# A mixer, convolution and MLP kernel: split forget gate, all high parts on ScalarE, another order in the first stage, the first swishes and the modulation

## The reference

```python
h = rms_norm(x, norm_w); proj = h @ w_in
gq, gk, gv, glr, hq, hf, hi, xq, gate = split(proj)
# heads 0-3: gated linear attention, gate from glr; m = rms_norm(mem, mem_norm_w), mk, mv = m @ w_mem_kv
# heads 4-7: the same recurrence; forget gate sigmoid(hf), key (1 - lb) * sigmoid(-hf)
# heads 8-11: cross attention of xq to mk, mv
mixed = concat(heads) * silu(gate)
x = rms_norm(x + mixed @ w_out, final_norm_w)
mod = silu(c) @ w_mod + b_mod            # shifts, scales and gates of the next two blocks
x = x + gate1 * conv_block(modulate(norm(x)))   # 1024->2048, GLU, 31-tap depthwise, LayerNorm, silu, 1024->1024
x = x + gate2 * mlp(modulate(norm(x)))          # hidden 4096
```

## Time and profile before

| | |
|---|---|
| time, median of 3 | 2173.16 us (2172.41 to 2177.71) |
| profiled execution, own time / span | 2175.57 / 2173.8 us |
| PE busy | 2060.9 us (95%) |
| DVE, ACT, POOL busy | 1077.7 (50%), 793.0 (36%), 808.0 (37%) us |
| mean granted PE clock | 0.968 of full speed |
| POOL's high parts, L2534 | 32 of 1134 ns, 36.3 us |
| ACT's high parts, L1715 | 173 of 1058 ns, 183.0 us |
| landing of MODRAW, median | 4.5 us after issue |

### The profile page before, as it was taken

One profiled execution on the slowest core, in us unless ns is written; L12 is line 12 of the kernel. 1 busy time (PEld: TensorE's weight loads), 2 busy tenths in 40 slices (PEclk: granted clock), 3 DMA queues, 4 the chain that ended last, 5 costly groups with the idle time before them and its releaser, 6 DMA issues. The chain is left out here.

```text
span 2173.8 us, 26461 instructions
## 1 busy us (share of the span) xinstructions
PE 2060.9 (95%) x10302; PEld 1727.4 (79%) x10302; DVE 1077.7 (50%) x1881; ACT 793.0 (36%) x1339; POOL 808.0 (37%) x481
## 2 busy tenths in 40 slices
PE   7899999999899899999899998899999999999997
PEld 5788988878887678888778776678777888888886
DVE  6364455446454255555569978994423122122125
ACT  4413221332434522132356556652425333312211
POOL 3342122122131344353238877663443444222220
PEclk9999999999999999999999999899899999999998
DMA  4211101011011486776245432123222333111112
GB/s 166 70 56 49 40 30 49 30 56 32 21 60 43 150 303 209 234 261 204 96 150 190 175 121 82 58 79 96 68 88 88 97 97 97 49 49 49 49 49 78
DMA packets 69420, 215.64 MB, mean 99 GB/s; under 512 B 7712, under 2 KB 8096, under 8 KB 69168
## 3 DMA queue, kind: packets, MB, share of 16 engines
q1 hardware_dynamic: 55184, 187.73, 25.2%
q10 hardware_dynamic: 14112, 26.22, 3.7%
HBM read 184.56 MB, written 29.36 MB: 98 GB/s over the span
## 5 line engine op out<-in xcount | busy, mean ns | idle before, releaser
L1320 PE MATMUL B<-HB,WH 128*128 128x512 f32 x2976 | 950.4, 406 | 28.6 <-ACT WH L1715 10.8
L2536 POOL TENSOR_TENSOR WL<-RAW,WH 128x1024 fp32r<-128x1024 f32 x205 | 496.3, 2424 | 686.2 <-ACT WH L1715 681.9
L1320 PEld LDWEIGHTS B<-HB,WH 128*128 128x128 f32 x2976 | 557.8, 192 | 151.7 <-issue 33.2
L1320 PE MATMUL B<-HB,WL 128*128 128x512 f32 x1488 | 574.1, 396 | 4.1 <-POOL WL L2536 4.0
L1715 ACT ACTIVATE WH<-RAW 128x1024 fp32r<-128x1024 f32 x173 | 183.0, 1058 | 460.8 <-DMA RAW<-wall 444.4
L1320 PEld LDWEIGHTS B<-HB,WL 128*128 128x128 f32 x1488 | 284.9, 191 | 68.2 <-POOL WL L2536 6.6
L2034 DVE SCALAR_TENSOR_TENSOR RES<-B,modv,RES 128x512 f32<-128x512 f32 x144 | 105.1, 748 | 207.6 <-PE B L1499 181.4
L2034 DVE SCALAR_TENSOR_TENSOR B<-UP,vec,B 128x512 f32<-128x512 f32 x308 | 207.4, 750 | 0.0
L1499 PE MATMUL B<-HIDH,WH 128*128 128x512 f32 x512 | 188.2, 401 | 6.5 <-DVE HIDL L2031 5.0
L1499 PE MATMUL B<-HIDL,WH 128*128 128x512 f32 x512 | 183.8, 392 | 0.0
L1499 PE MATMUL B<-HIDH,WL 128*128 128x512 f32 x512 | 183.6, 392 | 0.0
(11 more groups left out here) (240 smaller groups left out, 2688.6 us busy)
## 6 DMA issues: line engine op xcount, KB each, us to landing
RAW<-wall SPq DMA_DIRECT2D x203, 512.0 KB, 3.5
MODRAW<-wmod ACTq DMA_DIRECT2D x96, 256.0 KB, 4.5
WH<-parts SPq DMA_DIRECT2D x32, 512.0 KB, 3.2
WL<-parts SPq DMA_DIRECT2D x32, 512.0 KB, 4.2
RES<-xT SPq DMA_DIRECT2D x16, 512.0 KB, 8.2
oscr<-OT SPq DMA_DIRECT2D x32, 256.0 KB, 2.1
OI<-oscr SPq DMA_DIRECT2D x16, 512.0 KB, 5.2
parts<-WH SPq DMA_DIRECT2D x16, 512.0 KB, 5.2
```

Source lines behind the costliest of these rows:

```text
L1320: i = pe.matmul(bank, a[:, ks], hb(part, k, h), start=k == 0 and n == 0, stop=k == 7 and n == 2)
L2536: po.tensor_tensor(lo, raw, hi.bitcast(F32), ALU.subtract).then_inc(sig[f"w_lo{q % NW}"], 1)
```

## The change

Six edits. (1) The forget gate is two pieces: the sigmoids at once, the scalings 4.0 planner-us later, the head's recurrence 2.5 after that (it was 6.0 in one). (2) All high parts are made by ACT. (3) Stores of turned outputs are a piece of their own, 2.5 planner-us after the turning. (4) In the first stage 20 matmuls on a tile of ones run first (line 1640); the identity is waited for only where it is used; ACT starts one raw load instead of two; steps of the norms of x and mem come earlier or in another order, with double buffers for mem. (5) A gate block's B x R product is a piece `mix_r` of its own; the swishes of blocks 0 and 1 come after the product of block 2. (6) In blocks 4 to 8 `mods(4)` is put in after the first half too, so the 96 pieces run up to 20 ahead of where they stood.

```diff
-FORGET = 6.0
+FORGET = (4.0, 2.5)
-LATER = (2.5, 3.0, 3.0)
+LATER = (2.5, 3.0, 3.0, 2.5)
+WARM = 20
 def u_split():
-            piece("split", q, "act" if UNITS[q][0] in ("mk", "mv") else hi_by[0])
+            piece("split", q)
 def x_stats():
         take(S, "x_sum")
         piece("x_sum")
-        for _ in range(4):
-            yield
-        piece("x_diag")
         yield
         yield
+        piece("x_diag")
+        piece("m_square")
+        for _ in range(3):
+            yield
         for h in range(2):
             take(S, "x_row", h)
             piece("x_row", h)
         R_done[0] = True
+        yield
+        yield
+        for h in range(2):
+            piece("glr", h)
+        for h in range(2):
+            piece("q_out", 0, h)
...
 def turn():
+            while P.kinds["turn_o"] - P.kinds["ot_store"] > 4 - tiles:
+                next_due()
...
+            later(LATER[3], store)
...
 def recurrent(n):
-        piece("forget", n)
-        later(FORGET, lambda: bg.append(linear(n)))
+        piece("forget_sig", n)
+        def forget():
+            piece("forget", n)
+            later(FORGET[1], lambda: bg.append(linear(n)))
+        later(FORGET[0], forget)
...
-    def mix_out(e, h):
+    def mix_out(e, h, first=True):
+        if first:
+            piece("mix_r", e, h)
         piece("mix", e, h)
...
 def mixed(e):
             gate_product(e, h)
             mix_out(e, h)
+            if h == 0 and 4 <= e < 9:
+                mods(4)
...
     gate_product(1, 0)
-    crossed_up_to(1)
     for e, h in ((0, 0), (0, 1), (1, 0)):
-        mix_out(e, h)
+        piece("mix_r", e, h)
     gate_product(1, 1)
-    mix_out(1, 1)
-    for e, h in ((2, 0), (2, 1), (3, 0)):
-        gate_product(e, h)
+    piece("mix_r", 1, 1)
+    for h in range(2):
+        gate_product(2, h)
+    crossed_up_to(0)
+    for e, h in ((0, 0), (0, 1), (1, 0), (1, 1)):
+        mix_out(e, h, False)
+    for h in range(2):
+        piece("mix_r", 2, h)
+        gate_product(3, h)
...
 # PE program
-            w.wait_ge(sig["d_ident"], 16)
+            w.wait_ge(sig["ones"], 1)
+            for _ in range(WARM):
+                pe.matmul(BANKS[use["glr", 0][0]], ones[:, :].bitcast(F32R), ...)
 # SP program
             load_x(0)
             sp.dma_start(vec[:, :], vecs).then_inc(sig["d_vec"], 16)
+            load_x(1)
+            load(1)
+            for k in range(2, 8):
+                load_x(k)
             sp.dma_start(ident[:, :], ident_d).then_inc(sig["d_ident"], 16)
-            for k in range(1, 8):
-                load_x(k)
```

More of the change, by code:

```diff
@@ L180, in make_plan @@
     lanes = {"dve": [], "pool": []}
-    hi_by, ahead, pace = ["act"], [AHEAD], [PASS]
+    ahead, pace = [AHEAD], [PASS]
     def u_split():
@@ L356, in mem_norm @@
         yield
-        yield
-        yield
         piece("m_diag")
-        yield
+        for _ in range(3):
+            yield
         take(S, "m_row")
         piece("m_row")
+        for k in range(8):
+            yield
+            piece("m_tile", k)
     rate[0] = 0.8
@@ L382, in make_plan @@
         step()
+    step_in(bg2)
     for h in range(2):
-        piece("glr", h)
-    for h in range(2):
-        piece("q_out", 0, h)
         piece("k_out", 0, h)
@@ L403, in scale @@
             later(LATER[2], turn)
+        tiles = 2 if n < 4 else 1
         def turn():
-            for f in range(2 if n < 4 else 1):
+            while P.kinds["turn_o"] - P.kinds["ot_store"] > 4 - tiles:
+                next_due()
+            for f in range(tiles):
                 take(S, "turn_o", n, hh, f)
@@ L409, in turn, with store @@
             fin_n[n >= 8, hh] += 1
+            later(LATER[3], store)
+        def store():
+            for f in range(tiles):
+                piece("ot_store", n, hh, f)
         later(LATER[0], rms)
@@ L510, in make_plan @@
             piece("gate_up", h, hf)
+        if bg2:
+            step_in(bg2)
         piece("gate_log", h)
@@ L677, in make_plan @@
         after(2.5 * f, "res_load", f)
[L678 to L681, removed]
+    for h in range(2):
+        mix_out(2, h, False)
+    for h in range(2):
+        mix_out(3, h)
     mods(4)
@@ L1113, in build_program @@
         dg0 = at("p0dg", 1024, F32, x0 + 4 * K4)
-        macc, msq, mdg, mtm = (at(f"mem{i}", 256, F32, x0 + 8 * K4 + i * 1024) for i in range(4))
+        macc, mdg = (at(f"mem{i}", 256, F32, x0 + 8 * K4 + i * 1024) for i in range(2))
+        msq, mtm = ([at(f"mem{n}{i}", 256, F32, o + i * 1024) for i in range(2)]
+                    for n, o in (("sq", x0 + 6 * K4), ("tm", x0 + 8 * K4 + 2048)))
         mraw = at("mraw", 8 * 256, F32, x0 + 9 * K4)
@@ L1607, in pe_program @@
                         mean=mean, ysum=ysum, ln_row=ln_row)
-            w.wait_ge(sig["d_ident"], 16)
+            w.wait_ge(sig["ones"], 1)
+            for _ in range(WARM):
+                pe.matmul(BANKS[use["glr", 0][0]], ones[:, :].bitcast(F32R), ones[:, 0:1].to_broadcast([128, 512]).bitcast(F32R), start=True, stop=True)
             for kind, *a in P.order:
@@ L1719, in x_hi_lo, with split @@
                 copy(hb(0, k), xr[k], scale=vcol("norm_w", k)).then_inc(sig["x_hi"], 1)
[L1721 to L1726, removed]
+            def split(q):
+                w.wait_ge(sig[f"d_raw{q % NW}"], 16 * raw_n[q])
+                if q >= NW:
+                    wait_unit_read(w, q - NW)
+                copy(WH[:, slot(q)], RAW[:, slot(q)]).then_inc(sig[f"w_hi{q % NW}"], 1)
             def x_square(k):
@@ L1741, in m_square, with m_tile @@
                 for k in range(8):
-                    if k >= 2:
-                        w.wait_ge(sig["m_add"], k - 1)
-                    ac.activation((msq if k else macc)[:, :], mraw[:, k * 256:(k + 1) * 256],
+                    if k > 2:
+                        w.wait_ge(sig["m_add"], k - 2)
+                    ac.activation((msq[k % 2] if k else macc)[:, :], mraw[:, k * 256:(k + 1) * 256],
                                   ACT.Square).then_inc(sig["m_sq"], 1)
[L1747 to L1753, removed]
+            def m_tile(k):
+                if k < 7:
+                    w.wait_ge(sig["m_tm"], k + 1)
+                else:
+                    wait_taken(w, "m_row")
+                copy(mhl[0][:, k * 256:(k + 1) * 256], mtm[k % 2][:, :]).then_inc(sig["m_hi"], 1)
             def mk_out(h):
```

57 lines of the change are left out of this document (25 added, 32 removed).

## The result

| | before | after |
|---|---|---|
| median of 20 runs each | 2173.49 us (2162.91 to 2180.14) | 2180.47 us (2174.29 to 2185.60) |
| ratio after to before, 95% interval | | 1.0027 (1.0016 to 1.0037) |
| profiled execution, span | 2173.8 us | 2173.3 us |
| PE busy | 2060.9 us | 2059.2 us |
| POOL busy / ACT busy | 808.0 / 793.0 us | 771.5 / 817.8 us |

The change made the kernel slightly slower: 7.0 us in the medians, 5.9 us by the ratio. Forecast were 2181 us and +8. The profiled execution of after is one of its fastest (own time 2175.09 us, against a median of 2180.47). So the two profiles have equal spans: after is 3.9 us behind at the first product of the convolution and 0.5 us ahead at the end. The traces are used for where time goes, and the medians for how much it is in all.

The account below looks back on a forecast made before the run. PE is busy 95% of the span, so the change can act only on PE's waits and the clock behind them. Terms: -12 - 7 - 6 + 9 + 36 - 12 = +8 on 2173.2 gives 2181 us, range 2168 to 2200.

Parts of the forecast that it names:

- First stage: Start of the kernel: waits for mem and VB go with most of the slow clock, -12 us, bounds -4 and -15.
- the 1 us for the warm matmuls: Kernel start: 20 matmuls on ones bring first products to full speed; sum of x's squares comes about 1 us sooner.
- Forget gate: Heads 4 and 6: later scalings let ST's copy go sooner, shortening PE's waits for ST, -7 us, bounds -12 and -2.
- high parts: High parts moved from POOL to ACT: fewer collisions with DVE's products, shorter waits for AB, set1k, set0k, -6 us.
- OSB alone sets it: Forget gate's low bound, -2 us: ACT's copy OSB, still behind the sigmoids, alone sets the wait.
- The bound of -16: Far bound of the high parts' gain: all three waits (AB, set1k, set0k) go with their clock; other bound +5.
- Swishes: Cross attention's end: PT waits go, -5; four second products pile up on DVE, +10; block 4's pieces, +4; together +9 us.
- Pieces between the halves: Blocks 5 to 8: each half on DVE becomes a load round trip of 10.45 us, +36 us including 3.5 of clock.
- the quiet row's 7.7: Time in us from MXH's end to the last of four pieces in a quieter stretch, taken for each round trip.
- Last piece: End of the gate blocks: the 6.8 us wait for MACC and 5.1 us of clock go, -12 us, bounds -7 and -12.
- A short landing: First rival, blocks 5 to 8: with landings of 2.6 us a half costs 8.35, the term 16; 2161 us, chance 0.25.
- The second rival: Gains shrink (first stage -4, forget gate -2, collisions +3) while losses stand: +40, or 2213 us, chance 0.10.

Follow-up runs that it names:

- old swishes: After with the swishes of blocks 0 and 1 where they stood before, the rest kept: 2168.39 us, ratio to before 0.9967.
- first experiment: After without the pieces between the halves of blocks 4 to 8, everything else kept: 2148.53 us, ratio to before 0.9884.
- both cures: After with the loads of the next four pieces one triple sooner and the swishes of blocks 0 and 1 where they stood before: 2132.08 us, ratio to before 0.9812.
- the three with early loads and OSB not behind the swishes: After with early loads plus: old swishes (2132.08 us); those and the forget gate's sigmoids 1.0 planner-us later (2128.65); or OSB's scalings ahead of the second products (2129.61).
- early loads: After with the loads of the next four pieces one triple sooner in the plan, same loads, pieces and bytes: 2141.03 us, ratio to before 0.9848.

## Why the prediction was right

The time (2181 forecast, 2180.5 measured) is nearer than its terms deserve. The largest term was right in its mechanism and nearly in its size, but two errors of some 10 us each cancelled, and that is luck. The forecast +8 was worked out for the profiled executions; there the terms sum up to +3.9 us at the convolution and -0.5 at the end, and the +7 is in the medians alone. The prediction took 6.5 us as the least that can be told from no change, and gave no change 0.20; the ratio's 5.9 us lies below that, though its interval leaves out zero.

- *First stage, -12.* Measured -16.4 at no. 240: the waits for mem and VB went with their slow clock, as it said. The step that failed is the 1 us for the warm matmuls, which were to bring the first products to full speed: the clock had fallen again by then, and the kernel without them takes the same time. The other edits of this stage were not run singly.
- *Forget gate, -7, and high parts, -6.* In the traces the two and the later stores give -7.3 from no. 240 to 768 and -16.0 from there to 1152, of which -5 was forecast for the softmax rows (against the old swishes it is -2.9). Singly on the chip the forget gate is worth 3.3 us by the medians, half of the term, and not at the two waits that the term was made of: OSB on ACT ends last there, which was its bound "OSB alone sets it". High parts are worth 14 us, more than double. The bound of -16 held; what was missing is that collisions also hit OSB's scalings in heads 1 to 3, where the kernel before had no wait to show. The stores were not tested alone.
- *Swishes, +10 for the pile against the 5 won, and +4 for block 4.* Measured +12.8 by no. 1248 and +12.1 by 1344. The old swishes give back 12 us in all, the pieces of block 4 another 12 (first experiment). This is the term that was sized too small. The prediction had the pile's 10.2 us, but let block 3's products cover part of it; nothing did, since the turning of the last head stood in PE's order ahead of them and waited 11.6 us. For block 4 it counted a slower half. But the first wo product waits for the bank of the second half (9.3 us), whose `GA<-B,R` stood behind four pieces; these waited 6.75, 1.20, 1.20 and 0.77 us for their transfers and ended 12.9 us after the first was asked for.
- *Pieces between the halves, +36.* Measured +31.8 in the traces, 32 by leaving them out. A half cost DVE 9.8 us in the mean instead of 10.45: from the first issue to the last use the seven groups of blocks 5 to 8 took 6.6 to 9.7 us, about the quiet row's 7.7. The waits came where it said, MACC and then RES. Their sum is not what it said: 18.0 us of waits and 13.7 of slow clock, where it had 32.6 and 3.5 ("30 us in all" for the waits).
- *Last piece, -12.* Measured -12.1, and it came back as soon as the extra pieces were left out (+12.2).
- *Rivals.* A short landing did not come: the median landing was 4.4 us, and four pieces took 6.6 us at the least. The estimate from the fixed 2.0 us of the Trainium skill's page "DMA: Bandwidth & Descriptors" (section "Anatomy of one DMA — SWDGE (gpsimd) path") would have been 5.2 us; the measurement decides against it for four transfers from ACT's queue beside the weight stream. The second rival named OSB on ACT and POOL's subtractions: both mechanisms are real, but they made gains smaller or larger and turned no sign.

Behind the blocks, after makes up 3.2 us between the convolution and no. 3840, in a part that the change hardly touches. The clock record tells where: in before's profile the granted clock is 0.50 from 1629.8 to 1636.6 us, around a wait of 3.4 us for DG, and after's profile has the same wait and no such stretch. That differs from execution to execution: of two profiles of the kernel with both cures one has such a stretch (1583.9 to 1590.7 us) and the other has none. What stays open is where the medians' 7 us lie, since no profile of after is of a median execution.

The best version is any of the three with early loads and OSB not behind the swishes: 2128.7 to 2132.1 us, some 2% below the kernel before. Among themselves they can't be told apart.

## What to carry to other kernels

Before work is put in between two steps, ask where its loads stand in the issuing engine's order. Here 20 pieces brought forward won 12 us and cost 44 (the 32 by which after is slower than without them, and the 12), because each group was asked for right ahead of its use, and asking for it one triple sooner turned the loss into a gain. What hid the round trip here was the work that stood between the load and its use; DVE, half idle over the whole, waited all the same.

When work is postponed, look for the small instruction that now stands behind it (OSB's scalings), and for the engine that holds the next engine's bank.

## What the runs showed of the hardware

- Four loads of 256 KB, issued from ACT within 1.8 to 2.5 us, were used up 6.6 to 9.7 us after the first issue in blocks 5 to 8 of after, though the median landing of one is 4.4 us. In block 4, where the issue took 3.8 us and each landing 6.7 to 9.2, it was 12.9 us.
- Single-tile scalings on DVE were slower beside POOL: four of 128x256 took 6.47 us beside POOL's three instructions in a row and 3.26 us beside one; four of 128x128 took 3.98 us beside POOL's products and 0.87 us with POOL idle.
- In after 20 matmuls raised the granted clock to 1.00 at 4.8 us, and it was 0.50 again from 11.6 to 15.0, after idle times of 1.64 and 1.72 us. The run with early loads has the same first stage and kept 1.00 from 6.5 us on. Neither gained by it (2180.15 us without the 20 matmuls, 2180.47 with).
- With the same waits, the clock fell in one execution and not in another: 6.8 us at 0.50 around a wait of 3.4 us in before's profile, none in after's. So a difference of some 3 us between two single profiles need not come from an edit.
